# A two-layer diffusion trunk step on one core: the low-part products of each stage's first dense pair issued one chunk behind the high-part products

## The reference, cut to what matters

```python
def trunk_layer(x, mod, ..., mixer):
    shift1, scale1, gate1, shift2, scale2, gate2 = mod
    h = rmsnorm(x, g_mix_pre) * (1 + scale1) + shift1
    y, ctx_state = mixer(h)          # h @ w_in, attention, then (concatenated heads) @ w_out
    x = x + gate1 * rmsnorm(y, g_mix_post)
    h = rmsnorm(x, g_ffn_pre) * (1 + scale2) + shift2
    x = x + gate2 * rmsnorm(conv_ffn(h, w_ffn_in, w_ffn_conv, w_ffn_out), g_ffn_post)
    return x, ctx_state
```

## Time and profile before

| | us |
|---|---|
| median of 3 runs | 1830.66 |
| lowest and highest | 1830.52, 1837.47 |
| the profiled execution | 1832.45 |
| its span, first to last instruction | 1830.7 |
| PE busy | 1673.3 (91%) |
| DVE busy | 1099.8 (60%) |
| ACT busy | 723.0 (39%) |
| mean granted TensorE clock | 0.959 |

### The profile page before, as it was taken

The page is one execution under the profiler, slowest core; times in us unless marked ns, Lnnn a source line. Parts: engine busy times, 40 slices in busy tenths (PEclk is TensorE's granted clock), DMA queues, the critical chain, the costliest instruction groups (busy, mean ns, idle before and its releaser), DMA issues.

```text
span 1830.7 us, 33159 instructions
## 1 busy us (share of the span) xinstructions
PE 1673.3 (91%) x12232; PEld 1585.8 (87%) x12232; DVE 1099.8 (60%) x2058; ACT 723.0 (39%) x1187; POOL 137.8 (8%) x135
## 2 busy tenths in 40 slices
PE   5798599877999999999979979989889999999995
PEld 1697388877999999999979977779789999999995
DVE  4484766666777767777765227762466652466524
ACT  3721266326444214342151117663276541244410
POOL 1060310000000000000001023320000000000000
PEclk9899699988999999999989989999999999999998
DMA  8253000340334543335423220001112222122211
GB/s 291 88 161 91 8 2 2 127 150 20 118 103 127 184 160 104 114 112 183 153 71 101 59 72 2 24 23 47 46 46 69 80 91 71 63 75 73 86 59 58
DMA packets 42800, 160.70 MB, mean 88 GB/s; under 512 B 5088, under 2 KB 6112, under 8 KB 42336
## 3 DMA queue, kind: packets, MB, share of 16 engines
q1 hardware_dynamic: 39888, 152.00, 25.9%
q0 software_dynamic: 1616, 6.68, 1.1%
q10 hardware_dynamic: 1216, 0.92, 0.2%
HBM read 156.04 MB, written 3.54 MB: 87 GB/s over the span
## 4 chain that ended last, share of the span: by engine, by line
PE 76%; DVE 6%; issue 3%; ACT 2%; DMA 1%; DVEq 1%; ACTq 0%; SPq 0%
PE ps L1380 27%; PE ps L1381 27%; PE ps L1536 4%; PE ps L1565 4%; PE ps L1551 2%; PE ps L1433 2%; PE ps L1419 2%; PE ps L1491 2%; PE ps L1492 2%; DMA ring<-in_wmodt 1%; DVE x L892 1%; PE ps L1394 1%; PE ps L1393 1%; DVE ring L794 1%; PE ps L1552 1%
## 5 line engine op out<-in xcount | busy, mean ns | idle before, releaser
L497 ACT ACTIVATE whi<-raw 128x1024 fp32r<-128x1024 f32 (+1 forms) x166 | 185.6, 1121 | 615.6 <-PE ps L1381 520.6
L1380 PE MATMUL ps<-hh,whi 128*128 128x320 f32 x920 | 286.0, 311 | 9.9 <-DVE wlo L786 9.9
L1381 PE MATMUL ps<-hl,whi 128*128 128x320 f32 x920 | 284.6, 309 | 0.0
L1380 PE MATMUL ps<-hh,wlo 128*128 128x320 f32 x920 | 284.6, 309 | 0.0
L1381 PE MATMUL ps<-hh,wlo 128*128 128x320 f32 x920 | 284.6, 309 | 0.0
L1380 PE MATMUL ps<-hl,whi 128*128 128x320 f32 x920 | 284.6, 309 | 0.0
L1381 PE MATMUL ps<-hh,whi 128*128 128x320 f32 x920 | 284.6, 309 | 0.0
L786 DVE TENSOR_TENSOR wlo<-raw,whi 128x1024 fp32r<-128x1024 f32 (+1 forms) x166 | 218.9, 1321 | 74.6 <-ACT whi L497 74.4
L1380 PEld LDWEIGHTS ps<-hh,whi 128*128 128x128 f32 x920 | 173.1, 188 | 10.9 <-DVE wlo L786 10.9
L1380 PEld LDWEIGHTS ps<-hh,wlo 128*128 128x128 f32 x920 | 173.1, 188 | 0.0
L1381 PEld LDWEIGHTS ps<-hh,whi 128*128 128x128 f32 x920 | 173.0, 188 | 0.0
(11 more groups left out here) (210 smaller groups left out, 3347.7 us busy)
## 6 DMA issues: line engine op xcount, KB each, us to landing
raw<-in_w SPq DMA_DIRECT2D x134, 512.0 KB, 3.6
work<-in_wmodt SPq DMA_DIRECT2D x54, 512.0 KB, 3.7
raw<-in_w SPq DMA_DIRECT2D x32, 704.0 KB, 4.2
ring<-in_wmodt SPq DMA_DIRECT2D x26, 512.0 KB, 4.1
work<-in_wmod SPq DMA_DIRECT2D x16, 512.0 KB, 5.3
work<-in_rpb POOLq DMA_DIRECT2D x8, 480.0 KB, 4.6
x<-in_x SPq DMA_DIRECT2D x1, 2560.0 KB, 17.9
out_x<-x SPq DMA_DIRECT2D x8, 320.0 KB, 2.2
```

The source lines that it names most:

```text
L497: nc.scalar.activation(whi[:, s, 0:kk * P], raw[:, s, 0:kk * P], ACT.Copy).then_inc(s_hi, 1)
L1380: T.matmul(bankA[s], slot(w, s, k), h[:, k, 0:HT], start=st, stop=sp_)
L1381: last = T.matmul(bankB[s], slot(w, s, k), h[:, k, HT:NT], start=st, stop=sp_)
```

## The change

The chunk of a pair is cut in two. `pair_high(k)` issues the eight products of both slots with `hh` of chunk k, and waits for the high part alone. `pair_low(k)` issues the four products with `hl` of chunk k, behind `pair_high(k + 1)`, with a wait of its own for the low part. The products, their number and the PSUM banks are the same. `s_unit` is now given in `pair_low(7)`.

```diff
-            def pair_chunk(k):
+            def pair_high(k):
                 for s in range(2):
-                    for n, (w, h) in enumerate(((whi, hh), (whi, hl), (wlo, hh))):
-                        st, sp_ = k == 0 and n == 0, k == KD - 1 and n == 2
-                        T.matmul(bankA[s], slot(w, s, k), h[:, k, 0:HT], start=st, stop=sp_)
-                        last = T.matmul(bankB[s], slot(w, s, k), h[:, k, HT:NT], start=st, stop=sp_)
+                    for w in (whi, wlo):
+                        st = k == 0 and w is whi
+                        T.matmul(bankA[s], slot(w, s, k), hh[:, k, 0:HT], start=st, stop=False)
+                        T.matmul(bankB[s], slot(w, s, k), hh[:, k, HT:NT], start=st, stop=False)
+
+            def pair_low(k):
+                for s in range(2):
+                    T.matmul(bankA[s], slot(whi, s, k), hl[:, k, 0:HT], start=False, stop=k == KD - 1)
+                    last = T.matmul(bankB[s], slot(whi, s, k), hl[:, k, HT:NT], start=False, stop=k == KD - 1)
                     if k == KD - 1:
                         last.then_inc(s_unit, 1)
...
+            def first_pair(u0, h0):
+                pair_ready(u0)
                 for k in range(KD):
-                    pe.wait_ge(s_hl, hl0 + k + 3)
-                    pair_chunk(k)
+                    pe.wait_ge(s_hh, h0 + k + 1)
+                    pair_high(k)
+                    if k:
+                        pe.wait_ge(s_hl, h0 + k + 2)
+                        pair_low(k - 1)
+                pe.wait_ge(s_hl, h0 + KD + 2)
+                pair_low(KD - 1)
```

More of the change, by code:

```diff
@@ L1484, in dense_pairs, with pair_ready @@
                         dense(s, 2 * h + (u0 + s))
-            def pair_chunk(k):
+            def pair_high(k):
                 for s in range(2):
-                    for n, (w, h) in enumerate(((whi, hh), (whi, hl), (wlo, hh))):
-                        st, sp_ = k == 0 and n == 0, k == KD - 1 and n == 2
-                        T.matmul(bankA[s], slot(w, s, k), h[:, k, 0:HT], start=st, stop=sp_)
-                        last = T.matmul(bankB[s], slot(w, s, k), h[:, k, HT:NT], start=st, stop=sp_)
+                    for w in (whi, wlo):
[6 more added lines that the diff above has]
+                    last = T.matmul(bankB[s], slot(whi, s, k), hl[:, k, HT:NT], start=False, stop=k == KD - 1)
                     if k == KD - 1:
                         last.then_inc(s_unit, 1)
-            def first_pair(u0, hl0):
+            def pair_ready(u0):
                 pe.wait_ge(s_lo, u0 + 2)
@@ L1592, in mix_pair @@
             def mix_pair(layer):
[L1594 to L1597, removed]
+                pair_ready(UNITS[(layer, "mix")][0])
                 for k in range(KD):
-                    pe.wait_ge(s_otl, KD * layer + k + 1)
-                    pair_chunk(k)
+                    pe.wait_ge(s_oth, KD * layer + k + 1)
+                    pair_high(k)
+                    if k:
+                        pe.wait_ge(s_otl, KD * layer + k)
+                        pair_low(k - 1)
+                pe.wait_ge(s_otl, KD * layer + KD)
+                pair_low(KD - 1)
             mix_pair(0)
```

## The result

| | median us | lowest to highest | runs |
|---|---|---|---|
| before | 1833.37 | 1829.88 to 1838.77 | 22 |
| changed | 1839.08 | 1832.16 to 1842.19 | 22 |

The ratio is **1.0029, with a 95% interval of 1.0019 to 1.0039**: the changed kernel is slower by 5.3 us (3.5 to 7.1). That is under the 0.5% that the forecast called "within", but it is clear of zero, and 1839.08 lies above the range of 1827.5 to 1836.0. Part of the miss is the starting point: the three runs shown before the change had a median of 1830.66, while 22 runs have 1833.37. The size of the change is still wrong without that: +1.3 us was forecast, +5.3 us measured, closer to the +6.5 of the rival "the later release cools the PE". The forecast also said that a measurement of this kernel tells about 0.5% from no change; 22 runs of each kernel tell 0.1%.

A forecast was written before the change was run, and what follows sets the result against it. The PE, busy 91% of the span, was taken as the bound. -0.2 us without the clock plus 1.5 us from the clock gave +1.3 us: 1832.0 us against the median of 1830.66, range 1827.5 to 1836.0.

The forecast's parts named there:

- within: Whole kernel: the time changes by no more than 0.5%, between 1821.5 and 1839.8 us; chance 0.96.
- the later release cools the PE: Rival: behind pairs 2 to 5 the clock falls every time, nothing won ahead of pairs; +6.5 us, 1837.2 us; chance 0.20.
- The starts: Start of each pair: PE begins on the high part, 0.98 or 0.86 us earlier, 5.6 us in all.
- The later release: End of each pair: slot 0 is released with the 94th matmul, not the 90th, 0.59 us later against the pair's end.
- The gain handed back: All six pairs, clock left out: earlier starts nearly cancelled by what follows; -0.8 to +0.5 us, middle -0.2.
- No waiting within a pair: Inside each pair: chunks come every 2 us, so the PE does not starve and shows no idle time.
- The added waits: Inside each pair: 16 waits instead of 8, taken as 0; 1 us if each of 48 cost 0.02 us.
- The clock: Around the pairs: half-clock falls behind them, less one stretch spared at the front; net +1.5 us.
- 2 falls, +3.0 us: Behind the pairs: chance 2 in 5 for each of pairs 2 to 5, 1 in 5 more for 1 and 6; 1.5 us each.
- Six falls cost 9.2 at the very most: Behind all six pairs: the upper limit on the loss, used to argue against a change over 0.5%.
- The 1.5 us at the front: Ahead of pairs 2 and 5: shorter idle time shortens or spares a half-clock stretch, taken once, -1.5 us.

The follow-up runs named there:

- the filled changed kernel: The changed kernel with eight matmuls of 320 columns added behind each pair, into a PSUM bank nobody reads: 1832.33 us, 0.9997 of the kernel before.
- the release put back: The changed kernel with chunk 7 issued slot by slot, so slot 0 is released with the 90th matmul again: 1831.87 us, 0.9995 of the kernel before.
- the late release alone: The kernel before with only chunk 7 reordered, so slot 0 is released with the 94th matmul; starts and waits kept: 1840.41 us, ratio 1.0037.
- slot 0 first: The changed kernel with all of slot 0 ahead of slot 1 from chunk 6 (pairs 2 and 5: chunk 4) on: 1827.10 us, 0.9964 of before.
- the run with the warm start: Kernel issuing slot 0 ahead of slot 1 at pair ends, plus 12 matmuls ahead of pairs 1, 3, 4, 6 and five ahead of 2, 5: 1826.11 us, 0.9960.

## Why the prediction was right or wrong

**The starts, right.** They were to come 0.98 and 0.86 us earlier, the idle time ahead of the pairs to shrink from 22.1 to about 16.5 us. It is 3.22 + 1.63 + 3.34 + 3.33 + 1.58 + 3.34 = 16.4 us, released by the high parts.

**The later release, right.** The idle time behind the pairs grew by 0.59 us in pairs 2, 4, 5 and 6, to 2.35, 2.30, 2.35 and 3.57. That single edit, done alone, gave the whole loss.

**The gain handed back, right.** The sum without the clock was -0.8 to +0.5 us, middle -0.2. With the idle time filled in both kernels they stand at 0.9997 and 0.9998; the difference is 0 with some 3 us on either side. By pairs, 0 was forecast for pair 1 and +0.13 for pair 6, and the table of pairs shows 0.0 and +0.2. The -1.6 and -1.3 us of pairs 2 and 5 belong to the clock term, not to this sum. Where the half-clock stretch at the start of pair 2 is as long as before, in the filled changed kernel (3.4 us), the pair with its idle times takes 19.8 us against 19.9: -0.1, within the forecast of -0.27 to +0.12.

**No waiting within a pair, nearly right.** One wait for a high part stands in pair 1, 0.27 us long. The added waits cost nothing that could be seen.

**The clock, wrong, and here the sum broke.** The mechanism was the one forecast; the term was too small. The step was "2 falls, +3.0 us", less 1.5 us for a stretch spared at the front, "net of the clock: +1.5". The falls behind the pairs are worth 5.9 us by the filled run (with some 2.6 us on either side) and 5.4 us by the three stretches of the one profile. Two errors made the term too small. First, the number of falls. In the profiles of the unfilled kernels (before, changed, the release put back, the late release alone, each half of the change, and the other pairs of the run that filled pairs 3 and 6), the idle time behind pairs 2 to 6 stands against a fall like this:

| idle time behind the pair | pairs seen | with a half-clock stretch behind | of these 6.7 to 6.8 us long |
|---|---|---|---|
| 1.71 to 1.76 us | 11 | 0 | 0 |
| 2.30 to 2.35 us | 12 | 6 | 0 |
| 2.54 to 2.98 us | 7 | 4 | 2 |
| 3.57 us | 3 | 3 | 3 |

The table leaves out pair 1 and the kernels with slot 0 first, and both blur it. Behind pair 1 of the same kernels the clock fell after 3.49, 3.84, 4.07 and twice after 4.33 us, and did not after 3.25 and 3.29 us. With slot 0 first it stayed at 1.00 after 3.19 us (pair 1) and 2.10 us (pair 6); with the PE kept busy ahead of the pairs as well, it fell after 3.17 and 2.10 us in the same places. The length of the idle time alone doesn't decide it.

Two in five for pairs 2 to 5 was about right for an idle time of 2.3 us. But pair 3 didn't stay at 2.3: the PE finished its pair early and ACT, busy with the wide vector, did not, so the idle time was 2.82 us in the changed kernel:

```profile
450.59 1.91 ACT L599 ACTIVATE cwide<-cwide 128x2048 f32<-128x2048 f32 x1
```

The PE's last matmul of the pair starts at 451.63, and ACT takes up its weight copy at 452.41. I had named that and then priced pair 3 like the others. Second, and more, the price: I gave pair 6 one chance in five of 1.5 us. At 3.57 us of idle time it fell each time, for 6.7 to 6.8 us, of which 5.4 to 5.6 us were busy: 2.5 us each. "Six falls cost 9.2 at the very most" was wrong for the same reason. The trace of before already held the warning in the other direction, the 6.7 to 6.8 us stretches ahead of pairs, and I priced all falls behind them at the 3.4 us of the one case seen. Filling behind pairs 3 and 6 alone took back 3.8 of the 5.3 us in the middle of the intervals, which allow anything from 1 us to all of it.

**The 1.5 us at the front, too small by the profiles.** It was taken once. Of the seven profiles in which pairs 2 and 5 start on the high part with no fill ahead of them, pair 2 has no half-clock stretch at its start in five and 3.4 us in two; pair 5 has none in one and 3.4 us in six. In the four profiles with the old start pair 2 has 3.4 us in three and 6.8 us in one, and pair 5 has 6.8 us in all four. So about one stretch was spared in each of the two pairs, some 3 us in all (an estimate, at 1.5 us each), twice what was put down. If the times hold it too, the falls behind the pairs cost 5.3 + 0.2 + 3 = 8.5 us, at the edge of what the filled run allows; the balance isn't settled more closely than that. The times show only the net of this and of the falls behind the same pairs: 0.9991 with the change in pairs 2 and 5 alone, 1.6 us, with an interval that reaches 1.0001. In pair 6 the run with the warm start shows why nothing was to be had: the chunks bound the pair.

**The rival that came true.** "Slower: the later release cools the PE" had 0.20 and gave +6.5 us. Its mechanism is the one found; its place and count are not, so that its number came close is in part luck. It let the clock fall behind each of pairs 2 to 5; after 2.3 us it fell in half of the cases. It had nothing won ahead of the pairs and no cost behind pair 6; pairs 2 and 5 lose nothing that can be seen, and the loss is in the four pairs behind a norm. Behind pair 6 it is largest in the profiles; its share in the times is open.

**What stays open.** The profile of the changed kernel is 6.7 us longer than that of before. Of this, 3.2 us were won around the pairs and 5.4 lost behind them; 4.5 us lie in the stretch between pairs 1 and 2, where the time from pair to pair went from 258.7 to 263.3 us though pair 1 took the same. Over all twelve kernels profiled this stretch takes 258.6 to 263.6 us, high and low with and without the change (263.3 with the release put back, 258.6 with the changed kernel filled). Its length goes with the clock: it takes 234.7 to 235.6 us from behind pair 1 to pair 2 in the five profiles with 38 to 41 us at half clock in it, 237.2 to 237.4 in the three with 47.8, and 239.5 to 239.8 in the four with 51 to 52. The changed kernel's profile has a half-clock stretch at 152.0 us and one at 220.3 us, inside that work, that the profile of before lacks. No order of the pairs goes with them, so this looks like scatter of the execution; what sets it off was not tried. The other parts roughly cancel: the changed kernel's profile reaches pair 1 1.9 us sooner and spends 1.1 us more between pairs 5 and 6. All this makes single profiles a poor measure of a difference of 5 us.

## What to carry to other kernels

When an instruction order is changed to start earlier, look at which instruction gives the release at the other end: four matmuls moved ahead of it cost 0.37% by themselves and more than undid the earlier starts, and the last thing to be issued in a group should be what nobody waits for. An idle time on the PE has a price beyond its length once the clock falls, and then a gap that grows by 0.6 us can cost 2.5; a fill of a few matmuls on an unused bank is a cheap test of whether that is what is being paid. Where producers bound a stretch, as in pair 6, a warmer PE wins nothing there.

## What the runs showed of the hardware

Gaps with the same instructions around them behaved differently from profile to profile: behind pairs 2 to 6, with 2.30 to 2.35 us idle the clock fell in 6 of 12 cases, with 1.71 to 1.76 us in none of 11. I had expected a fall to last 3.4 us, as in the one case of the trace before; behind 3.57 us it lasted 6.8. In the changed kernel's pair 6 the clock was low from 1353.6 on, 1.2 us before the PE resumed at 1354.76, and stayed low for 5.5 us of dense work. Added up over all six pairs of one profile, the half-clock time behind the pairs was 17.0 us in the changed kernel, 13.6 us with the late release alone and 23.8 us with the change in the norm pairs alone (1.0029, 1.0037 and 1.0041), against 3.4 us before and 6.8 us with the release put back or with the idle time filled (0.9995 and 0.9997). With the change in pairs 2 and 5 alone it was 6.8 us at 0.9991. With only pairs 3 and 6 filled it was 13.6 us at 1.0008, in a profile where it fell behind pairs 1, 4 and 5: one profile is one throw of these falls, and the ratios rest on the times.
